# A two-layer hybrid block on one core: weight splits moved into the pair work, column sums folded on VectorE, y scaled on ScalarE, ada units moved

## The chip, the core and the metric

The kernel runs on 1 core of one Trainium2 chip. The time is that of one execution on the device, in microseconds. Below, the median of three runs is given, and beside it one execution that was taken with the hardware profiler. Times inside that execution count from the start of its span.

## What is computed

Two layers, on 512 tokens of 1024 channels, in fp32. Each layer is a mixer and a feed-forward part, each between two RMS norms and gated by values made from a condition vector c.

```python
def reference(...):
    c_act = jax.nn.silu(c)
    for l in range(DEPTH):
        mod = (c_act @ ada_w[l] + ada_b[l]).reshape(bsz, N_MOD, D_MODEL)[:, :, None, :]
        shift_m, scale_m, gate_m = mod[:, 0], mod[:, 1], mod[:, 2]
        shift_f, scale_f, gate_f = mod[:, 3], mod[:, 4], mod[:, 5]
        h = rms_norm(x, mix_pre_g[l]) * (1.0 + scale_m) + shift_m
        y = hybrid_mixer(h, ...)            # w_in, attention and RG-LRU, w_out
        x = x + gate_m * rms_norm(y, mix_post_g[l])
        h = rms_norm(x, ffn_pre_g[l]) * (1.0 + scale_f) + shift_f
        y = conv_ffn(h, ffn_w_up[l], ffn_conv_w[l], ffn_conv_b[l], ffn_w_down[l])
        x = x + gate_f * rms_norm(y, ffn_post_g[l])
    return x

def conv_ffn(h, w_up, conv_w, conv_b, w_down):
    u = causal_dwconv(h @ w_up, conv_w, conv_b)      # width 3 over time, 2 * 3072 channels
    g, val = jnp.split(u, 2, axis=-1)
    return (jax.nn.gelu(g, approximate=True) * val) @ w_down
```

## The kernel before

Channels lie on partitions in eight tiles, time (512) along the free dimension. A fp32 product is made of three fp32r products: of weight and activation each a high part (rounded) and a low part (the rest), high by high, high by low, low by high. The weights come as a stream of chunks of 128x1024, 512 KB each: per layer 14 for `w_in`, 8 for `w_out`, then three groups of 16 up chunks (gate and value alternate) and 8 down chunks. A chunk is loaded by SyncE into a ring of six slots (`refill`, L460, each load waits until the chunk six places before it has been used), ScalarE makes the high part (`split_step`, L595, into `wH`), and VectorE the low part (`lo_chunk`, L1149, in place as `wL`). The last two out chunks and the last two down chunks of each layer have side buffers of their own.

Every engine's order is written out by hand, and the engines meet by counting semaphores. TensorE's products are `half_products` (L1894, one half of 256 tokens) and `tile_products` (through `mm`, L1869, all 512). The out stage, the first six chunks of the up group and the last six down chunks are done in halves, so that the norms of the first half go on while TensorE does the second half. Two chunks of such a stage share one PSUM bank and are called a pair.

The places that the change touches:

- **Pair work.** The six chunks `U0` to `U0 + 5` are the gate and value chunks of three pairs. For each half h and pair p, ScalarE evicts both (`pair_base`, L828), VectorE adds the taps of the convolution (`pair_taps`, L1612 and L1614), ScalarE makes the gelu (`pair_gelu`, L836), VectorE the product (`pair_product`, L1629), ScalarE its high part (`pair_high`, L842) and VectorE its low part (`pair_low`, L1638). The prediction counts up chunks from one: chunk seven is `U0 + 6`, the first that is done in one piece. The splits of chunks seven to eleven stand between these steps, on ScalarE and VectorE alike. They are asked for by `ring_next(U0 + c, SLOTS_W - 1)`, the chunk five places on.
- **The later up chunks** run through a loop (`f_base`, L1049; taps, L1733 and L1736; gelu, L1045; high part, L1055; low part, L1745). A down chunk waits for the high and low part of each of its eight tiles.
- **Ada units.** `mod` is made in layer 0 for both layers, by VectorE: a unit is one row block of `ada_w`, 512 KB, fetched by GpSimd (L563), multiplied with c and summed (`dot_unit`, L1155). The table `UNITS` says after which chunk each unit is done.
- **Post norm.** The squares of y are summed over the tiles in `sum_of[h]`, whose 512 columns hold two sets of 256 tokens side by side (for the down stage tiles 0 and 1 are in `sum_full`). `post_early` on TensorE sums them over the partitions with matmuls against a column of ones (`half_sums`, L1994), 128 tokens at a time; `post_final` does the same with the last pair's squares. Then come ScalarE's root (`post_root`, L621), VectorE's reciprocal (L1199), and `post_spread`, which spreads the factor over the partitions (L1869). A matmul of plain fp32 is two instructions in the trace.
- **x_update** (L1205 to L1215) multiplies y by that factor and adds it to x, four tiles at a time. In the out stage y has been scaled by `fac` in its eviction, so one multiply does it (L1209); in the down stage `fac` is applied here, tile by tile (L1212). In the last layer the result is stored by SyncE (L511).

```python
for p in range(3):
    if p == 0:
        split_step(ring_next(U0 + 1, SLOTS_W - 1))
    pair_base(1, p)
    for c in range(2 * p, 2 * p + 2):
        if c > 1:
            split_step(ring_next(U0 + c, SLOTS_W - 1))
    pair_gelu(1, p)
    pair_high(1, p)
```

Of the kernel before, what the change touches and what calls it, by code (L numbers as in the profile page):

```python
# [25 lines left out]
P = 128  # L26
# [71 lines left out]
def build(nc, A):  # L98
# [3 lines left out]
    with ctx:  # L102
# [29 lines left out]
        side_raw = [at(f"side{i}", [P, KT * P], top[0] - (2 - i) * KT * SEQ * 4 + 4 * SEQ * 4) for i in range(2)]  # L132
        raw_at = top[0]
# [158 lines left out]
        fac_ready, last_ready = sem("fac_ready"), sem("last_ready")  # L292
# [51 lines left out]
        def norm_half(l, k, h):  # L344
            return 2 * (2 * l + k) + h + 1

# [66 lines left out]
        for _g in range(GROUPS):  # L413
            for _p in range(GRP // 2 if _g == 0 else 0, KT):
                _n = 2 if _g == 0 and _p < GRP else 1
                UNITS[up_no(_g, 2 * _p + 1)] = list(range(_u, _u + _n))
                _u += _n
# [25 lines left out]
        def _(sp):  # L443
# [63 lines left out]
            for h in range(2):  # L507
                for q in range(2):

                    sp.wait_ge(x_half, 2 * (norm_half(DEPTH - 1, 1, h) - 1) + q + 1)  # L510
                    sp.dma_start(out4[:, 4 * q:4 * q + 4, part_of(h)],  # L511
                                 x4[:, 4 * q:4 * q + 4, part_of(h)]).then_inc(stored, 16)
            sp.wait_ge(stored, 16 * 4)
# [70 lines left out]
        def _(act):  # L584
# [119 lines left out]
            for l in range(DEPTH):  # L704
# [98 lines left out]
                def out_evict(h, i):  # L803

                    if h == 0 and i == 0:
                        act.wait_ge(fac_ready, l + 1)
# [214 lines left out]
                pair_base(0, 2)  # L1021
                pair_gelu(0, 2)
# [3 lines left out]
                for p in range(3):  # L1026
                    if p == 0:
                        split_step(ring_next(U0 + 1, SLOTS_W - 1))
                    pair_base(1, p)
                    for c in range(2 * p, 2 * p + 2):  # L1030
                        if c > 1:
                            split_step(ring_next(U0 + c, SLOTS_W - 1))
# [31 lines left out]
                N0 = B + NCH  # L1064
                act.wait_ge(dn_read, dn_no(l, GROUPS - 1, 0))
# [5 lines left out]
                split_step(D0 + 7)  # L1071

                def down_squares(h, i):
# [10 lines left out]
                    else:  # L1084
                        nc.scalar.activation(two(last_sq[h]), src, ACT.Square).then_inc(last_ready, 1)

# [45 lines left out]
        def _(dve):  # L1132
# [44 lines left out]
            def factors(l, which):  # L1177
# [8 lines left out]
                else:  # L1186
                    link(TT(fac[:, l, which, :], m, g, ALU.mult))

            def add_square(l, k, s, h):
# [3 lines left out]
                dve.wait_ge(sq_used, add_no(l, k, s))  # L1193

# [6 lines left out]
            def x_update(l, k, h, q):  # L1201
# [6 lines left out]
                if k == 0:  # L1208
# [6 lines left out]
                TT(xs, xs, ys, ALU.add).then_inc(x_half, 1)  # L1215
# [120 lines left out]
            for l in range(DEPTH):  # L1336
# [313 lines left out]
                dve.sem_inc(post_summed, 1)  # L1650
# [17 lines left out]
                dve.sem_inc(post_summed, 1)  # L1668
# [844 lines left out]
```

## Time and profile before

| | |
|---|---|
| median of 3 runs | 1194.88 us (1192.77 to 1198.26) |
| the profiled execution | 1199.15 us |
| its span, first to last instruction | 1197.3 us |
| mean granted TensorE clock | 0.981 of full |
| TensorE matmul busy | 1165.3 us, 97% |
| TensorE weight load busy | 1016.3 us, 85% |
| VectorE busy | 821.9 us, 69% |
| ScalarE busy | 544.4 us, 45% |
| GpSimd busy | 52.1 us, 4% |
| read from HBM | 152.64 MB, 129 GB/s over the span |

The time of an execution is a little more than its span. A busy share is an average over stages: what ends a wait at one place is read from the timeline there. "PE" is TensorE, "DVE" VectorE, "ACT" ScalarE, "POOL" GpSimd and "SPq" SyncE's DMA issues. An entry in brackets at the end of a timeline row gives the idle time of the engine just before it, and what ended that.

### The profile page before, as it was taken

Reading aid. Unit: us, or ns where it says so; the run is one execution under the profiler, and the core shown is the slowest. Engines: PE = TensorE matmul, PEld = TensorE weight load, DVE = VectorE, ACT = ScalarE, POOL = GpSimd, SP = SyncE. Lnnn points to the kernel's source line nnn. Section 1 sums busy time; section 2 is a strip of 40 time slices with the busy share of each in tenths; the row PEclk is TensorE's granted clock in tenths of the full one; section 3 lists DMA queues with packets and bytes.
Section 4 is the critical chain, followed back from the end, with each engine's and each line's share of the span. In section 5 each row is a group of like instructions: output and inputs, shape, how many; then the busy total and the mean of one; then the engine's idle time right before and its main releaser. Section 6 shows DMA issues by size and latency. Waiting matters only on the chain.

```text
span 1197.3 us, 16181 instructions
## 1 busy us (share of the span) xinstructions
PE 1165.3 (97%) x6616; PEld 1016.3 (85%) x6616; DVE 821.9 (69%) x1267; ACT 544.4 (45%) x896; POOL 52.1 (4%) x110
## 2 busy tenths in 40 slices
PE   6999999989999999999999999998999999999996
PEld 6986899978788888888999779997888888888896
DVE  7899867688777777677487885577653666356634
ACT  5388726454224431444248874545432444234430
POOL 4000110000110011000000000000000000000000
PEclk8999889999999999999999999999999999999998
DMA  9833533235775458544113220304333333333312
GB/s 361 344 107 110 188 120 128 86 118 191 248 255 158 140 190 285 177 140 141 42 48 106 71 87 20 106 5 140 104 92 102 91 103 92 102 92 102 92 50 71
DMA packets 44938, 155.79 MB, mean 130 GB/s; under 512 B 5056, under 2 KB 7360, under 8 KB 44864
## 3 DMA queue, kind: packets, MB, share of 16 engines
q1 hardware_dynamic: 34352, 116.48, 29.5%
q0 software_dynamic: 10368, 37.75, 9.4%
q8 instruction: 52, 0.85, 0.3%
q10 hardware_dynamic: 144, 0.52, 0.1%
q14 instruction: 22, 0.18, 0.1%
HBM read 152.64 MB, written 2.10 MB: 129 GB/s over the span
## 4 chain that ended last, share of the span: by engine, by line
PE 80%; DVE 13%; ACT 4%; issue 2%; DMA 1%; SPq 0%; DVEq 0%
PE ps L1869 57%; PE ps L1894 21%; PE ps L1994 2%; DVE sb_wL L1149 2%; DVE sb_R L1614 1%; DVE sb_stage L1155 1%; ACT sb_R L828 1%; ACT sb_wH L595 1%; DVE sb_R L1736 1%; DVE sb_R L1733 1%; DVE sb_y L1233 1%; ACT sb_sq L700 1%; DVE sb_xc L1381 0%; DVE sb_adaw L1155 0%; DMA sb_raw<-in_w 0%
## 5 line engine op out<-in xcount | busy, mean ns | idle before, releaser
L1869 PE MATMUL ps<-sb_hH,sb_wH 128*128 128x512 f32 x800 | 315.3, 394 | 7.6 <-DVE sb_wL L1149 7.6
L1869 PE MATMUL ps<-sb_hH,sb_wL 128*128 128x512 f32 x800 | 312.1, 390 | 0.0
L1869 PE MATMUL ps<-sb_hL,sb_wH 128*128 128x512 f32 x800 | 311.9, 390 | 0.0
L595 ACT ACTIVATE sb_wH<-sb_raw 128x1024 fp32r<-128x1024 f32 x174 | 181.5, 1053 | 127.8 <-DMA sb_raw<-in_w 127.7
L1149 DVE TENSOR_TENSOR sb_wL<-sb_raw,sb_wH 128x1024 fp32r<-128x1024 f32 x174 | 211.7, 1219 | 30.3 <-ACT sb_wH L595 30.1
L1869 PEld LDWEIGHTS ps<-sb_hH,sb_wH 128*128 128x128 f32 x800 | 150.5, 188 | 42.0 <-DVE sb_wL L1149 9.1
L1869 PEld LDWEIGHTS ps<-sb_hL,sb_wH 128*128 128x128 f32 x800 | 150.6, 188 | 31.6 <-issue 1.0
L1869 PEld LDWEIGHTS ps<-sb_hH,sb_wL 128*128 128x128 f32 x800 | 150.5, 188 | 31.7
L1733 DVE SCALAR_TENSOR_TENSOR sb_R<-ps,sb_par,sb_R 128x511 f32<-128x511 f32 x84 | 62.9, 748 | 100.9 <-ACT sb_R L1049 100.7
L1049 ACT ACTIVATE sb_R<-ps,sb_par 128x512 f32<-128x512 f32 x84 | 65.2, 777 | 116.1 <-PE ps L1869 116.1
L1869 PE MATMUL ps<-sb_mH,sb_wH 128*128 128x512 f32 x288 | 112.1, 389 | 0.9 <-ACT sb_mH L1055 0.9
L1869 PE MATMUL ps<-sb_mL,sb_wH 128*128 128x512 f32 x288 | 112.2, 389 | 0.0
L1869 PE MATMUL ps<-sb_mH,sb_wL 128*128 128x512 f32 x288 | 112.1, 389 | 0.0
L1894 PE MATMUL ps<-sb_hH,sb_wH 128*128 128x256 f32 x384 | 104.3, 290 | 0.1
L1894 PE MATMUL ps<-sb_hH,sb_wL 128*128 128x256 f32 x384 | 102.9, 287 | 0.0
L1894 PE MATMUL ps<-sb_mH,sb_wH 128*128 128x256 f32 x320 | 94.6, 296 | 0.2 <-ACT sb_adaw L769 0.2
L1894 PE MATMUL ps<-sb_mL,sb_wH 128*128 128x256 f32 x320 | 92.4, 289 | 0.0
L1894 PE MATMUL ps<-sb_mH,sb_wL 128*128 128x256 f32 x320 | 92.4, 289 | 0.0
L1894 PE MATMUL ps<-sb_hL,sb_wH 128*128 128x256 f32 x384 | 80.9, 285 | 1.2 <-DVE sb_hL L1240 1.2
L1894 PEld LDWEIGHTS ps<-sb_hH,sb_wH 128*128 128x128 f32 x384 | 75.3, 196 | 0.2 <-issue 0.2
L1894 PEld LDWEIGHTS ps<-sb_hH,sb_wL 128*128 128x128 f32 x384 | 75.3, 196 | 0.0
L1055 ACT ACTIVATE sb_mH<-sb_I 128x512 fp32r<-128x512 f32 x42 | 26.5, 632 | 100.7 <-DVE sb_I L1743 100.7
(253 smaller groups left out, 1750.1 us busy)
## 6 DMA issues: line engine op xcount, KB each, us to landing
sb_raw<-in_w SPq DMA_DIRECT2D x174, 512.0 KB, 3.6
sb_adaw<-in_ada POOLq DMA_DIRECT2D x42, 512.0 KB, 4.7
sb_stage<-in_ada SPq DMA_DIRECT2D x24, 512.0 KB, 14.3
sb_vw<-in_ada POOLq DMA_DIRECT2D x20, 512.0 KB, 4.9
sb_side<-in_w SPq DMA_DIRECT2D x8, 512.0 KB, 4.9
sb_raw<-in_w SPq DMA_DIRECT2D x8, 384.0 KB, 14.3
sb_stage<-in_ada POOLq DMA_DIRECT2D x6, 512.0 KB, 4.1
sb_x<-in_x SPq DMA_DIRECT2D x4, 512.0 KB, 5.3
```

The lines of the kernel that those rows point to most:

```text
L595: nc.scalar.activation(high_of(n), raw_of(n), ACT.Copy).then_inc(w_hi, 1)
L700: last = nc.scalar.activation(swaps[rope_no(l, h, i) % 2][32 * q4:32 * q4 + 32, cols], pair_bank(h, i)[32 * o:32 * o + 32, cols], ACT.Copy)
L828: last = nc.scalar.activation(R[:, c % 4, part_of(h)], pair_bank(h, p)[:, (c % 2) * HALF:(c % 2 + 1) * HALF], ACT.Identity, bias=pcol(l, " ...
L1049: nc.scalar.activation(R[:, c % 4, :], bank(up_bank(u)), ACT.Identity, bias=par_l[:, COLS["fcb"] + col:COLS["fcb"] + col + 1], scale=pcol( ...
L1055: nc.scalar.activation(mH[:, p, :], I[:, 2 + p % 2, :], ACT.Copy).then_inc(act_hi, 1)
L1149: TT(low_of(n), raw_of(n), high_of(n).bitcast(fp32), ALU.subtract).then_inc(w_lo, 1)
L1155: STT(out=tile, in0=tile, scalar=1.0, in1=csb[:, :], op0=ALU.mult, op1=ALU.mult, accum_out=mod[:, seg, kt:kt + 1]).then_inc(ada_used, 1)
L1233: STT(out=yt(j)[:, part_of(h)], in0=xt(j)[:, part_of(h)], scalar=gains[:, j:j + 1], in1=bank(X_BANK[h])[:, 0:HALF], op0=ALU.mult, op1=ALU. ...
L1733: link(STT(out=buf[:, 1:], in0=acc[:, 0:SEQ - 1], scalar=pcol(l, "fcw", 2 * PAIRS + col), in1=buf[:, 1:], op0=ALU.mult, op1=ALU.add))
L1869: return nc.tensor.matmul(out, a, b, start=start, stop=stop, **kw)
L1894: return nc.tensor.matmul(out, a, b, start=start, stop=stop, skip_group_check=True)
L1994: return nc.tensor.matmul(out, a, b, start=start, stop=stop, skip_group_check=True)
```

## The change

Five things, all in the order or the operands of instructions.

1. On ScalarE and VectorE the split of chunk seven goes from behind the third pair of the first half to before its gelu (ScalarE) and before its product (VectorE). Chunk eight goes to the first pair of the second half, chunk nine stays with the second, ten and eleven stay with the third.
2. For the first halves (and the last layer's last half) VectorE adds `sum_full` (down stage) and the right 256 columns of `sum_of` onto the left 256 before TensorE sums over the partitions. `half_sums` then runs over one set of columns, and the matmuls on `sum_full` fall away.
3. In the last layer's down stage ScalarE writes y times `fac` into `scaled` (over hH and hL) beside its squares, and `x_update` has one multiply per four tiles instead of four.
4. The last half is stored in four pieces of two tiles instead of two of four, and its adds are split likewise.
5. Four ada units move from the first group's up chunks to the second's: pairs 4 to 8 of group 0 carried 2, 2, 2, 1, 1 and now carry 0, 1, 1, 1, 1; the first four pairs of group 1 now carry two each instead of one.

```diff
+        scaled = [at(f"scaled{i}", [P, 4, SEQ], top[0] - (2 - i) * KT * SEQ * 4) for i in range(2)]
...
+        def folded(l, k, h):
+
+            return h == 0 or (k == 1 and l == DEPTH - 1)
...
-            for _p in range(GRP // 2 if _g == 0 else 0, KT):
-                _n = 2 if _g == 0 and _p < GRP else 1
+            for _p in range(KT // 2 if _g == 0 else 0, KT):
+                _n = 2 if _g == 1 and _p < KT // 2 else 1
...
-            for h in range(2):
-                for q in range(2):
-
-                    sp.wait_ge(x_half, 2 * (norm_half(DEPTH - 1, 1, h) - 1) + q + 1)
-                    sp.dma_start(out4[:, 4 * q:4 * q + 4, part_of(h)],
-                                 x4[:, 4 * q:4 * q + 4, part_of(h)]).then_inc(stored, 16)
-            sp.wait_ge(stored, 16 * 4)
+            halves = 2 * (norm_half(DEPTH - 1, 1, 0) - 1)
+            for q in range(2):
+                sp.wait_ge(x_half, halves + q + 1)
+                sp.dma_start(out4[:, 4 * q:4 * q + 4, part_of(0)], x4[:, 4 * q:4 * q + 4, part_of(0)]).then_inc(stored, 16)
+            for q in range(4):
+                sp.wait_ge(x_half, halves + 2 + q + 1)
+                sp.dma_start(out4[:, 2 * q:2 * q + 2, part_of(1)], x4[:, 2 * q:2 * q + 2, part_of(1)]).then_inc(stored, 16)
+            sp.wait_ge(stored, 16 * 6)
...
-                        act.wait_ge(fac_ready, l + 1)
+                        act.wait_ge(fac_ready, 2 * l + 1)
...
                 pair_base(0, 2)
+                split_step(ring_next(U0 + 1, SLOTS_W - 1))
                 pair_gelu(0, 2)
...
                 for p in range(3):
-                    if p == 0:
-                        split_step(ring_next(U0 + 1, SLOTS_W - 1))
                     pair_base(1, p)
-                    for c in range(2 * p, 2 * p + 2):
-                        if c > 1:
-                            split_step(ring_next(U0 + c, SLOTS_W - 1))
+                    for c in ((2,), (3,), (4, 5))[p]:
+                        split_step(ring_next(U0 + c, SLOTS_W - 1))
                     pair_gelu(1, p)
...
+                def scale(j, part):
+
+                    if l == DEPTH - 1:
+                        nc.scalar.activation(scaled[j // 4][:, j % 4, part], yt(j)[:, part], ACT.Copy,
+                                             scale=fac[:, l, 3, j:j + 1]).then_inc(y_scaled, 1)
...
+                if l == DEPTH - 1:
+                    act.wait_ge(fac_ready, 2 * l + 2)
+                scale(0, slice(0, SEQ))
+                scale(1, slice(0, SEQ))
...
                         nc.scalar.activation(two(last_sq[h]), src, ACT.Square).then_inc(last_ready, 1)
+                    scale(2 + 2 * i, part_of(h))
+                    scale(3 + 2 * i, part_of(h))
...
+            def all_added(l, k, h):
+
+                if folded(l, k, h):
+                    first = sum_of[h][:, 0:HALF]
+                    if k == 1:
+                        link(TT(first, first, sum_full[:, part_of(h)], ALU.add))
+                    link(TT(first, first, sum_of[h][:, HALF:2 * HALF], ALU.add))
+                dve.sem_inc(post_summed, 1)
...
-                if k == 0:
+                final = k == 1 and l == DEPTH - 1
+                if final:
+                    ys = scaled[q][:, :, part_of(h)]
+                    dve.wait_ge(y_scaled, 2 + 6 * h + (2 if q == 0 else 6))
+                if k == 0 or final:
                     V.mark(TT(ys, ys, rb.unsqueeze(1).broadcast_to([P, 4, HALF]), ALU.mult))
...
-                TT(xs, xs, ys, ALU.add).then_inc(x_half, 1)
+                if final and h:
+                    for j in range(2):
+                        two = slice(2 * j, 2 * j + 2)
+                        TT(xs[:, two, :], xs[:, two, :], ys[:, two, :], ALU.add).then_inc(x_half, 1)
+                else:
+                    TT(xs, xs, ys, ALU.add).then_inc(x_half, 1)
...
                 add_square(l, 0, 1, 0)
-                dve.sem_inc(post_summed, 1)
+                all_added(l, 0, 0)
...
-                half_sums(h, 0, sum_of[h], k == 1, False)
-                if k == 1:
+                half_sums(h, 0, sum_of[h], k == 1, False, 1 if folded(l, k, h) else 2)
+                if k == 1 and not folded(l, k, h):
```

VectorE's pair work gets the same new places with `lo_chunk` for `split_step`; `all_added` stands wherever `post_summed` was raised.

ScalarE in layer 0, from the eviction of the first half's third pair on, before (`sb_wH` is a split, `w_in2` the slot of chunk seven, `w_in3` that of eight; two evictions, gelu and high part make a pair):

```order
L828 ACTIVATE sb_R<-ps,sb_par 128x256 [waits p_mul,half_done]
L828 ACTIVATE sb_R<-ps,sb_par 128x256
L836 ACTIVATE sb_I<-sb_R 128x256 [waits p_taps]
L842 ACTIVATE sb_mH<-sb_I 128x256 [waits p_mul]
L1025 DMA sb_gw<-in_gw 128x1024
L595 ACTIVATE sb_wH<-sb_raw 128x1024 [waits w_in2]
L828 ACTIVATE sb_R<-ps,sb_par 128x256 [waits chunk_done]
L828 ACTIVATE sb_R<-ps,sb_par 128x256
L836 ACTIVATE sb_I<-sb_R 128x256 [waits p_taps]
L842 ACTIVATE sb_mH<-sb_I 128x256 [waits p_mul]
L828 ACTIVATE sb_R<-ps,sb_par 128x256 [waits chunk_done]
```

and in the change:

```order
L834 ACTIVATE sb_R<-ps,sb_par 128x256 [waits p_mul,half_done]
L834 ACTIVATE sb_R<-ps,sb_par 128x256
L601 ACTIVATE sb_wH<-sb_raw 128x1024 [waits w_in2]
L842 ACTIVATE sb_I<-sb_R 128x256 [waits p_taps]
L848 ACTIVATE sb_mH<-sb_I 128x256 [waits p_mul]
L1032 DMA sb_gw<-in_gw 128x1024
L834 ACTIVATE sb_R<-ps,sb_par 128x256 [waits chunk_done]
L834 ACTIVATE sb_R<-ps,sb_par 128x256
L601 ACTIVATE sb_wH<-sb_raw 128x1024 [waits w_in3]
L842 ACTIVATE sb_I<-sb_R 128x256 [waits p_taps]
L848 ACTIVATE sb_mH<-sb_I 128x256 [waits p_mul]
```

The split of chunk seven has passed one gelu and one high part, and that of chunk eight stands one pair earlier.

VectorE at the end of the last layer, from the last add of squares on, before (`sb_scr` is `sum_of[1]` and, in its right half, `sum_full`):

```order
L1192 TENSOR_TENSOR sb_scr<-sb_scr,sb_sq 128x512 [waits sq_ready]
L1775 TENSOR_TENSOR sb_y<-ps,sb_y 128x2x256 [waits sq_used,chunk_done]
L1199 RECIPROCAL sb_tiny<-sb_tiny 128x2 [waits post_sd]
L1212 SCALAR_TENSOR_TENSOR sb_y<-sb_y,sb_fac,ps 128x256 [waits post_rb]
L1212 SCALAR_TENSOR_TENSOR sb_y<-sb_y,sb_fac,ps 128x256 x3
L1215 TENSOR_TENSOR sb_x<-sb_x,sb_y 128x4x256 [waits dve_self]
```

and in the change:

```order
L1210 TENSOR_TENSOR sb_scr<-sb_scr,sb_sq 128x512 [waits sq_ready]
L1218 TENSOR_TENSOR sb_scr<-sb_scr 128x256 [waits sq_used]
L1219 TENSOR_TENSOR sb_scr<-sb_scr 128x256 [waits dve_self]
L1809 TENSOR_TENSOR sb_y<-ps,sb_y 128x2x256 [waits dve_self,chunk_done]
L1226 RECIPROCAL sb_tiny<-sb_tiny 128x2 [waits post_sd]
L1240 TENSOR_TENSOR sb_scaled_62<-sb_scaled_62,ps 128x4x256 [waits y_scaled,post_rb]
L1249 TENSOR_TENSOR sb_x<-sb_x,sb_scaled_62 128x2x256 [waits dve_self]
L1249 TENSOR_TENSOR sb_x<-sb_x,sb_scaled_62 128x2x256
```

Two folding adds stand ahead of the last pair's own add, one multiply stands for four, and two adds for one. The second group of four tiles follows in the same way.

## Rows read from the trace of the kernel before

**Rows 1.** The page: busy time by engine, and the chain that ended last.

```profile
PE 1165.3 (97%) x6616; PEld 1016.3 (85%) x6616; DVE 821.9 (69%) x1267; ACT 544.4 (45%) x896; POOL 52.1 (4%) x110
...
PE 80%; DVE 13%; ACT 4%; issue 2%; DMA 1%; SPq 0%; DVEq 0%
```

**Rows 2.** Waits of TensorE: us in total, times, longest us.

```profile
PE ps L1869 <- DVE sb_wL L1149: 7.6, 4, 2.2
...
PE ps L2129 <- DVE sb_mL L1429: 1.5, 1, 1.5
PE ps L1894 <- DVE sb_hL L1240: 1.2, 2, 1.1
```

**Rows 3.** Timeline, pair work of layer 0: start us, us, engine, line, operation.

```profile
233.75 1.01 ACT L828 ACTIVATE sb_R<-ps,sb_par 128x256 f32<-128x256 f32 x2
236.61 0.42 ACT L836 ACTIVATE sb_I<-sb_R 128x256 f32<-128x256 f32 x1 [1.85 <-DVE sb_R L1614]
...
237.94 1.06 ACT L595 ACTIVATE sb_wH<-sb_raw 128x1024 fp32r<-128x1024 f32 x1
...
240.31 0.50 PE L1869 MATMUL ps<-sb_hH,sb_wH 128*128 128x512 f32 x1 [1.63 <-DVE sb_wL L1149]
...
244.65 2.00 ACT L595 ACTIVATE sb_wH<-sb_raw 128x1024 fp32r<-128x1024 f32 x2
...
247.00 2.35 DVE L1149 TENSOR_TENSOR sb_wL<-sb_raw,sb_wH 128x1024 fp32r<-128x1024 f32 x2
...
248.27 0.50 PE L1869 MATMUL ps<-sb_hH,sb_wH 128*128 128x512 f32 x1 [2.20 <-DVE sb_wL L1149]
```

**Rows 4.** Line L460, loads issued at 230.8 and, fourth of the burst, 233.0.

```profile
DMA to landing us min/median/max: 3.7/3.7/3.7
...
DMA to landing us min/median/max: 6.2/6.2/6.2
```

**Rows 5.** Windows: us, then busy by engine, TensorE's granted clock, DMA share, GB/s.

```profile
238.70:254.05 15.35, 11.53 (x49) 9.23 (x50) 12.48 (x32) 8.91 (x16) 0.00 (x0) 1.00 0.37 126
254.05:264.93 10.88, 10.88 (x49) 9.01 (x48) 8.79 (x12) 5.86 (x9) 0.00 (x0) 1.00 0.30 97
297.56:304.42 6.86, 5.98 (x25) 4.35 (x25) 5.50 (x8) 3.23 (x5) 0.53 (x1) 1.00 0.44 153
814.50:831.30 16.80, 13.13 (x49) 10.36 (x50) 14.10 (x34) 8.74 (x16) 0.00 (x0) 0.90 0.23 77
...
823.90:827.30 3.40, 3.39 (x9) 2.73 (x10) 2.43 (x6) 1.94 (x4) 0.00 (x0) 0.59 0.17 69
138.60:158.90 20.30, 20.25 (x94) 19.13 (x95) 8.63 (x17) 6.06 (x13) 3.14 (x6) 0.50 0.41 144
```

**Rows 6.** First group of layer 0: the chain in order of time, then TensorE's timeline.

```profile
275.56 1.14 DVE sb_vw L1155 x2
...
285.87 1.14 DVE sb_adaw L1155 x2
...
303.17 0.50 PE L1869 MATMUL ps<-sb_mH,sb_wH 128*128 128x512 f32 x1 [0.88 <-ACT sb_mH L1055]
```

**Rows 7.** First half's sums, layer 0 down stage: the chain, then VectorE's timeline.

```profile
588.27 1.23 PE ps L1994 x12
...
588.31 0.69 DVE L1775 TENSOR_TENSOR sb_y<-ps,sb_y 128x512 f32<-128x512 f32 x1 [3.67 <-PE ps L1894]
```

**Rows 8.** Timeline of the tail, layer 0's out stage at 185.45, and the last store.

```profile
185.45 1.22 DVE L1209 TENSOR_TENSOR sb_y<-sb_y,ps 128x1024 f32<-128x1024 f32 x1 [1.19 <-PE ps L1869]
...
1186.50 0.26 ACT L621 ACTIVATE sb_tiny<-ps,sb_tiny 128x2 f32<-128x2 f32 x1 [1.14 <-PE ps L1994]
...
1188.27 1.66 DVE L1212 SCALAR_TENSOR_TENSOR sb_y<-sb_y,sb_fac,ps 128x256 f32<-128x256 f32 x4 [1.31 <-PE ps L1869]
1189.96 1.23 DVE L1215 TENSOR_TENSOR sb_x<-sb_x,sb_y 128x1024 f32<-128x1024 f32 x1
...
DMA to landing us min/median/max: 2.9/2.9/2.9
```

More of the change, by code:

```diff
@@ L291, in build @@
         post_rs, post_rb = sem("post_rs"), sem("post_rb")
-        fac_ready, last_ready = sem("fac_ready"), sem("last_ready")
+        fac_ready, last_ready, y_scaled = sem("fac_ready"), sem("last_ready"), sem("y_scaled")
         x_half, xsq_ready, x_summed = sem("x_half"), sem("xsq_ready"), sem("x_summed")
@@ L1187, in factors @@
                     link(TT(fac[:, l, which, :], m, g, ALU.mult))
+                    dve.sem_inc(fac_ready, 1)
             def add_square(l, k, s, h):
@@ L1667, in _ @@
                 add_square(l, 0, 3, 1)
-                dve.sem_inc(post_summed, 1)
+                all_added(l, 0, 1)
                 tmp_half(l, 0, 0, 2)
@@ L1712, in _ @@
                 pair_taps(0, 2)
+                lo_chunk(ring_next(U0 + 1, SLOTS_W - 1))
                 pair_product(0, 2)
@@ L1715, in _ @@
                 for p in range(3):
-                    if p == 0:
-                        lo_chunk(ring_next(U0 + 1, SLOTS_W - 1))
                     pair_taps(1, p)
-                    for c in range(2 * p, 2 * p + 2):
-                        if c > 1:
-                            lo_chunk(ring_next(U0 + c, SLOTS_W - 1))
+                    for c in ((2,), (3,), (4, 5))[p]:
+                        lo_chunk(ring_next(U0 + c, SLOTS_W - 1))
                     pair_product(1, p)
@@ L1790, in _ @@
                 add_square(l, 1, 1, 0)
-                dve.sem_inc(post_summed, 1)
+                all_added(l, 1, 0)
                 down_half(0, 2)
@@ L1799, in _ @@
                     add_square(l, 1, 2, 1)
-                    dve.sem_inc(post_summed, 1)
+                    all_added(l, 1, 1)
                     down_half(1, 2)
@@ L1815, in _ @@
                 add_square(l, 1, 2, 1)
-                dve.sem_inc(post_summed, 1)
+                all_added(l, 1, 1)
                 x_recip(l, 1, 0)
@@ L1994, in part_mm, with half_sums @@
                 return nc.tensor.matmul(out, a, b, start=start, stop=stop, skip_group_check=True)
-            def half_sums(h, at_, src, opens, closes):
+            def half_sums(h, at_, src, opens, closes, parts=2):
                 for t in range(2):
-                    for g in range(2):
+                    for g in range(parts):
                         first = g * HALF + t * P
                         last = part_mm(bank(STAT_BANK[h])[:, at_ + t:at_ + t + 1], src[:, first:first + P], ones[:, 0:1],
-                                       opens and t == 0 and g == 0, closes and g == 1)
+                                       opens and t == 0 and g == 0, closes and g == parts - 1)
                 return last
```

## Prediction

> **What bounds the kernel now.** I read the page's busy shares and chain first, then the waits of TensorE, then its timeline around each wait, then the windows. TensorE is busy for 1165.3 of 1197.3 us, and 80% of the chain that ended last is its own work [rows 1]. So time is won where TensorE stands still, where its clock is low, and where it runs matmuls that another engine could replace; work saved elsewhere counts only in the tail, after the last product. The largest wait is for one line, the low split of a weight chunk: 7.6 us in 4 waits, two per layer [rows 2].
>
> The timeline of layer 0 shows why [rows 3]. TensorE reaches up chunk seven at 238.68 and waits 1.63 us. ScalarE rounded its weights at 237.94 only, though the chunk's load, issued at 230.8, had landed after 3.7 us, at 234.5 [rows 4]: the split stood behind gelu and high part of the third pair. Then TensorE waits 2.20 us for chunk eight: ScalarE splits eight and nine together at 244.65, after the second pair's eviction, and VectorE ends the low split of eight at 248.2 (the row at 247.00 holds both). The data had been there for long, so both are waits for a place in ScalarE's order. Layer 1 repeats them.
>
> **Part 1, the splits.** The honest price is the time that two chunks take. From the end of chunk six to that of chunk eight (SyncE's loads mark these ends) layer 0 needs 15.35 us; the next two chunks need 10.88, or 5.44 each [rows 5]. Lost: 4.47. In layer 1 it is 16.80, lost 5.92, of which some 1.6 is the clock: after the second wait TensorE is granted 0.59 for 3.4 us [rows 5], which is mostly 1.2 instead of 2.4 GHz. Together 10.4 us; besides waits and clock, each restart costs a few tenths.
>
> Do the waits vanish or only move? I replay layer 0 with the durations of its rows. ScalarE ends the eviction of the third pair at 234.76 [rows 3], and the chunk is there (234.5). Split of seven 234.7 to 235.7; VectorE ends this pair's taps at 236.6 as before, then the low split to 237.7. Needed at 238.68: 1.0 us to spare. Product, high and low part of the pair follow 1.1 us later than they did. Eviction of the second half's first pair to 239.5, split of eight to 240.4, taps to 241.9, low split to 243.0; needed at 238.68 + 5.44 = 244.1. Next pair: low split of nine ends 248.2, needed at 249.6. Then ten at 253.4 for 255.0, eleven at 254.6 for 260.4. The least margin is 1.0 us. What is queued behind the moved split is the gelu of the same pair, which in both kernels waits for the taps until 236.61 anyway [rows 3]. Term: **10.4 us**; bounds 5 (one wait of each pair reappears) and 10.4.
>
> **Part 2, units moved.** In layer 0 each ada unit takes 1.14 us of VectorE, and a pair of chunks with two of them 10.3 us, from 275.56 to 285.87 [rows 6]. Before, three pairs of the first group carry two units, and VectorE stays behind until TensorE waits at 303.17 for the last high part, 0.88 us [rows 6]; that down chunk takes 6.86 instead of 5.44 [rows 5], so 1.42 is lost. Four units leave this group: 4 x 1.14 = 4.6 us of VectorE, and its first step starts 1.1 us earlier by the replay. The high part would be ready 5.7 us earlier, and TensorE needs it 4.47 us earlier. So it just fits, with a margin near 1.2 - 0.88 = 0.3 us. Term: **1.4 us**; bounds 0 and 1.4. The four units land in group 1, where four pairs now carry two. Such a pair takes VectorE 10.3 us against TensorE's 10.88 [rows 5, 6]: no new wait. GpSimd's fetches of the same units wait for their slots and move with them; two per pair of chunks is less than the two per chunk of the down chunks.
>
> **Part 3, column sums.** A sum matmul is issued as two passes: twelve instructions take 1.23 us, 0.10 apiece [rows 7]. Folding takes away 4 instructions in the out stage and 8 in the down stage, in each of 2 layers: 24 x 0.10 = **2.4 us** on TensorE. The last layer's second half loses 8 too, but there TensorE waits for the square of the last pair anyway: nothing. VectorE gains one add of 128x256 per out stage and two per down stage, some 0.4 us each as half of the 0.69 for 128x512 [rows 7]. Their cover is VectorE's pause of 3.67 us before the next half pair [rows 7]; without it they would delay the root and all that follows by 0.4 to 0.9 us a time. Bounds of the term: 1.5 and 2.5.
>
> **Part 4, the tail.** After the last spread everything is on the path: per group of four tiles 1.66 us of scaling and 1.23 of adding, twice [rows 8]. With y scaled beforehand the scaling is one multiply, as in the out stage, 1.22 [rows 8]: 0.44 saved each time. Each add becomes two, which costs an extra start: four pieces take 1.66 where one takes 1.22, so about 0.1 each. Net 0.7. ScalarE's two new scalings of the last pair stand ahead of its root; the eviction of two 128x256 pieces at 233.75 took 1.01 [rows 3], and ScalarE pauses 1.14 us there [rows 8]: hidden, barely. If they take longer, the excess is on the path. The last store holds 256 instead of 512 KB. 512 KB landed after 2.9 us [rows 8]; four loads issued within 2.2 us landed after 3.7 to 6.2 us [rows 4], so about 1.55 apart, which is what 512 KB costs in flow. Half is 0.75; the store before it, 0.6 earlier, takes back 0.1. Saved 0.65. Term: **1.3 us**, bounds 0.3 and 2.
>
> The loads of [rows 4] overlap everything but the flow of data, and two more stores should do so too. The Trainium skill, DMA: Bandwidth & Descriptors, Anatomy of one DMA, speaks against more and smaller transfers: it gives each about 2.0 us of fixed cost beside its bytes. Paid one after another, by its figures the last store would land 1.7 us later than now, and the sum would be 13.2.
>
> **Sum.** 10.4 + 1.4 + 2.4 + 1.3 = 15.5 us. Against the profiled execution (span 1197.3, time 1199.15) this gives 1183.6. The median of the runs shown is 4.3 lower, 1194.88. Whether the clock fell in layer 1 in those runs too is not known, so I take half of the 1.6: 14.7, and **1180.2 us**. Its own range is 1177 to 1183.5.
>
> **Rivals.**
> A, the waits move on. The replay has 1.0 us to spare, and loads further back in a burst landed up to 2.5 us later than the first [rows 4]; a late one now holds the whole pair work of ScalarE. Half of the 10.4 returns: 1185.4. For it: the thin margins. Against: the first of the burst is the one in question, and all later chunks have more.
> B, the last two stores run one after another with their whole 2.9 us each [rows 8]: the last lands 2 x 2.9 - 0.6 = 5.2 us after its issue, 2.3 later than now, where I counted 0.65 earlier. The sum is 12.6, the time 1183.1. Against it: the overlap in [rows 4].
> C, the clock. In this trace TensorE runs at 0.50 from 138.60 to 158.90 [rows 5]; at full clock that work would take half, so 10.2 us. It followed a wait of 1.5 us [rows 2], while a wait of 1.63 at 240.31 [rows 3] cost no clock. The change moves nothing there, but shifts all that follows, and waits remain, as at 643 us for the second half's hL [rows 2]. One such stretch more: 1190.4. The Trainium skill, TensorE: Matmul & The Clock Gate, Part 1, says that where the clock changes differs between runs of one kernel. One execution with a profile can neither bear that out nor refute it.
> D, the other side. The same mechanism in layer 1 behind 643 us, where scores, transposes and projections alternate with pauses until 720. Each stretch costs 10.2; two leave the kernel at 1200.6, within half a per cent of before, and slower by over 0.5% begins at 20.7 us lost. Three give 1210.8. Against: this part ran at 1.00 before, and its own order does not change.
> That the change doesn't do what it says is hardly open: the instruction order shows the splits ahead of gelu, and the sums gone.
>
> **Chances.** Forecast 0.72, A 0.14, B 0.04, C 0.07, D 0.03. A measurement of this kernel can tell about 0.5% from no change, 6.0 us, so faster means below 1188.9: forecast, A and B, 0.90. C is the same, 0.07, D slower, 0.03. The range of 1176.5 to 1187.5 takes in A and B, the smaller bounds of parts 2 to 4, and the upper side of the clock; C and D stay out.
>
> **What would show it.** Right: TensorE's waits for the low split at chunks seven and eight gone in both layers, two chunks in 10.9 us there, clock 1.00 in the first group of layer 1; no wait at the first down chunk of layer 0; first-half sums of 2 + 4 and 4 instructions instead of 10 and 12; two scaling multiplies of 1.22 at the end, and a last landing near 2.2 us after its issue. Wrong: a wait of over 1 us for chunks seven to eleven (part 1), one near the last high part (part 2), a root of the last half later than 1.1 us after its sums (part 4), or a new stretch below full clock.

## The result, and the profile after

| | before | changed |
|---|---|---|
| median of 6 runs | 1197.25 us (1192.77 to 1202.89) | 1185.53 us (1174.32 to 1187.11) |
| ratio, 95% interval | | 0.988 (0.983 to 0.993) |
| the profiled execution | 1199.15 us | 1174.32 us |
| its span, granted clock | 1197.3 us, 0.981 | 1172.5 us, 0.992 |

The change is faster by 1.2%, 0.7 to 1.7%. The forecast of 1180.2 us lies 5.3 below the median, inside its range of 1176.5 to 1187.5. But the two profiled executions are 24.8 us apart and the medians 11.7, where the sum said 15.5. Both deviations come mainly of stretches in which TensorE's clock is at half, and which differ from execution to execution; five of the twelve experiments are about them.

The page of the changed kernel:

```profile
PE 1149.5 (98%) x6584; PEld 1003.1 (86%) x6584; DVE 823.1 (70%) x1265; ACT 550.0 (47%) x910; POOL 51.9 (4%) x110
...
PE 90%; DVE 7%; ACT 1%; issue 1%; DMA 1%; SPq 0%; DVEq 0%
```

TensorE has 32 instructions fewer than in [rows 1]: the 24 first-half sums of part 3 and the 8 of the last half. Its own work is 90% of the chain now, against 80.

Its waits (us in total, times, longest):

```profile
PE ps L2163 <- DVE sb_mL L1465: 1.5, 1, 1.5
PE ps L2028 <- ACT sb_sqo L1100: 1.1, 1, 1.1
PE ps L1928 <- DVE sb_hL L1276: 1.1, 1, 1.1
```

The 7.6 us for `wL` in [rows 2] are gone. The 1.1 us for `sqo` stands where the last half's sums did; it is the tail's wait for the last squares, foreseen under part 3.

The timeline of layer 0's pair work, three engines (start us, us, engine, line, operation), beside [rows 3]:

```profile
224.61 1.00 ACT L834 ACTIVATE sb_R<-ps,sb_par 128x256 f32<-128x256 f32 x2
225.51 1.06 ACT L601 ACTIVATE sb_wH<-sb_raw 128x1024 fp32r<-128x1024 f32 x1
...
227.35 1.22 DVE L1166 TENSOR_TENSOR sb_wL<-sb_raw,sb_wH 128x1024 fp32r<-128x1024 f32 x1
...
227.46 0.42 ACT L842 ACTIVATE sb_I<-sb_R 128x256 f32<-128x256 f32 x1 [0.90 <-DVE sb_R L1650]
...
229.38 0.40 PE L1903 MATMUL ps<-sb_hH,sb_wH 128*128 128x512 f32 x1
...
230.27 1.06 ACT L601 ACTIVATE sb_wH<-sb_raw 128x1024 fp32r<-128x1024 f32 x1
...
232.64 1.22 DVE L1166 TENSOR_TENSOR sb_wL<-sb_raw,sb_wH 128x1024 fp32r<-128x1024 f32 x1
```

The split of chunk seven follows the eviction at once. Its low part ends at 228.57, and TensorE begins the chunk at 229.38 with no wait: 0.8 us to spare, where the replay had 1.0. The gelu still waits 0.90 us for the taps, so the split in front of it delays nothing.

Windows (us, then busy by engine, TensorE's granted clock, DMA share, GB/s): chunks seven and eight of layer 0, the next two, the first down chunk, seven and eight of layer 1, and the stretch at 139 us.

```profile
229.58:240.49 10.91, 10.91 (x49) 9.01 (x48) 8.55 (x23) 5.97 (x12) 0.00 (x0) 1.00 0.53 182
240.49:251.37 10.88, 10.88 (x49) 9.01 (x48) 9.45 (x18) 5.88 (x9) 0.00 (x0) 1.00 0.28 97
284.01:289.50 5.49, 5.49 (x25) 4.42 (x24) 4.16 (x6) 3.09 (x5) 0.00 (x0) 1.00 0.50 185
798.19:809.10 10.91, 10.91 (x49) 9.01 (x49) 8.55 (x23) 5.96 (x12) 0.00 (x0) 1.00 0.43 149
138.60:158.90 20.30, 19.97 (x170) 19.37 (x170) 16.32 (x30) 11.17 (x20) 3.66 (x7) 1.00 0.44 157
```

Against [rows 5]: 15.35 and 16.80 us are now 10.91 each, 6.86 is 5.49, and the stretch at 139 us ran at 1.00 in this execution where the one before ran at 0.50.

The chain in layer 0's down stage has the first half's sums, twelve in [rows 7], as

```profile
573.35 0.34 PE ps L2028 x4
```

And the tail, VectorE and ScalarE, with the landing of the last store, beside [rows 8]:

```profile
1163.43 0.26 ACT L627 ACTIVATE sb_tiny<-ps,sb_tiny 128x2 f32<-128x2 f32 x1 [0.34 <-PE ps L2028]
...
1164.79 1.22 DVE L1240 TENSOR_TENSOR sb_scaled<-sb_scaled,ps 128x1024 f32<-128x1024 f32 x1 [0.89 <-PE ps L1903]
1166.04 1.29 DVE L1249 TENSOR_TENSOR sb_x<-sb_x,sb_scaled 128x512 f32<-128x512 f32 x2
...
DMA to landing us min/median/max: 2.3/2.3/2.3
```

The root still waits for TensorE, by 0.34 us: ScalarE's two scalings are hidden, barely. The multiply takes 1.22 instead of 1.66.

**Where the 24.8 us went.** Aligned by SyncE's loads, the two spans differ by 9.7 in the part of layer 0 that holds the stretch at 139 us and the out stage (9.3 of it clock, 0.4 the out stage's sums), 4.4 and 5.9 in the pair works, 1.4 at the first down chunk, 0.9 + 0.4 + 0.9 in the other three first-half sums, and 1.75 in the tail; the start took 0.6 more. (The 0.4 of layer 0's out stage is taken from layer 1's, where no clock fall hides it.) The terms of the prediction are thus 16.1 of the 24.8, and the clock at 139 us is 9.3, which no part of the change addresses.

### The profile page after: what moved, and what is told of

Same layout as the page of the kernel before. It is cut to its first block, busy times and chain, and to the rows that moved or that the text cites. A ratio compares the mean times of both kernels' runs of the same rounds, so it can differ in the third digit from the quotient of the medians.

```text
span 1172.5 us, 16135 instructions
## 1 busy us (share of the span) xinstructions
PE 1149.5 (98%) x6584; PEld 1003.1 (86%) x6584; DVE 823.1 (70%) x1265; ACT 550.0 (47%) x910; POOL 51.9 (4%) x110
## 4 chain that ended last, share of the span: by engine, by line
PE 90%; DVE 7%; ACT 1%; issue 1%; DMA 1%; SPq 0%; DVEq 0%
PE ps L1903 64%; PE ps L1928 24%; PE ps L2028 2%; DVE sb_stage L1172 1%; DVE sb_wL L1166 1%; DMA sb_raw<-in_w 1%; ACT sb_sq L706 1%; DVE sb_xc L1417 1%; DVE sb_tiny L1399 0%; PE ps L2163 0%; ACT sb_scr L706 0%; DVE sb_scr L1303 0%; DVE sb_mL L1465 0%; DVE sb_R L1430 0%; DMA sb_sq<-in_pos 0%
## 6 DMA issues: line engine op xcount, KB each, us to landing
sb_raw<-in_w SPq DMA_DIRECT2D x8, 384.0 KB, 14.4
```

## The experiments

All runs have their own executions of the kernel before beside them on the same chip: with those of the result 64 in all, 1190.7 to 1202.9, median 1197.7 (the ratios are each against its own). The change had 12 executions in two runs, median 1185.4; where a run is compared with "the change" below, it is with these or with the profiled one.

**Each part alone: the splits back.** The change with the old places of the splits on both engines:

```diff
-                split_step(ring_next(U0 + 1, SLOTS_W - 1))
                 pair_gelu(0, 2)
...
                 for p in range(3):
+                    if p == 0:
+                        split_step(ring_next(U0 + 1, SLOTS_W - 1))
                     pair_base(1, p)
-                    for c in ((2,), (3,), (4, 5))[p]:
-                        split_step(ring_next(U0 + c, SLOTS_W - 1))
+                    for c in range(2 * p, 2 * p + 2):
+                        if c > 1:
+                            split_step(ring_next(U0 + c, SLOTS_W - 1))
```

> The changed kernel with the splits of chunks seven to eleven where they were. Theory (the terms add, each wait is one for its place in the order): TensorE waits again for chunk seven, some 1.5 us, and chunk eight, some 2.2 us, in both layers; from the end of chunk six to that of eight 15 us instead of 10.9 in layer 0 and 15 to 17 in layer 1; 9 to 10.4 us slower than the change at the same clock. Rival (the clock): the gain of the changed kernel came mainly from a stretch at half clock that it happened not to have; then this kernel is slower by under 4 us at the same clock. Of the first down chunk of layer 0: with the units moved but TensorE late again it must not wait.

Measured: 1194.58 us (10 runs), ratio 0.998 (0.995 to 1.001): without the splits hardly anything of the gain is left that a median can tell. The waits are back, in both layers; the windows are chunks seven and eight of each, then the first down chunk of layer 0:

```profile
235.11:250.42 15.31, 11.54 (x49) 9.23 (x50) 12.47 (x32) 8.89 (x16) 0.00 (x0) 1.00 0.38 124
809.58:824.77 15.19, 11.50 (x49) 9.23 (x50) 12.46 (x32) 8.76 (x16) 0.00 (x0) 1.00 0.26 89
293.94:299.38 5.44, 5.44 (x25) 4.50 (x24) 3.52 (x5) 3.04 (x4) 0.00 (x0) 1.00 0.33 108
```

The pair works took 4.40 and 4.28 us more than in the change, 8.7 together, at a clock of 1.00 in both. That is a little under the 9 to 10.4 expected at equal clock, and far above the rival's 4. The rest of the 10.4 is the fall of the clock in layer 1 of [rows 5], which did not occur in this execution. The first down chunk takes 5.44 without a wait, where [rows 5] had 6.86: beside the old splits the moved units are worth 1.42.

**The units back.**

```diff
-            for _p in range(KT // 2 if _g == 0 else 0, KT):
-                _n = 2 if _g == 1 and _p < KT // 2 else 1
+            for _p in range(GRP // 2 if _g == 0 else 0, KT):
+                _n = 2 if _g == 0 and _p < GRP else 1
```

> The changed kernel with the old table of units (2, 2, 2, 1, 1 for the last five pairs of group 0). Theory: TensorE is 4.4 us further ahead than before, VectorE gains 1.1 us only, so the wait for the last high part at the first down chunk of layer 0 is not 0.9 but some 4.3 us, and that is the whole loss: 4 to 5 us slower than the change at the same clock. Rival (the unit term is its own 1.4 us, whatever the splits do): 1.4 us slower.

Measured: 1190.3 us (10 runs), ratio 0.994 (0.991 to 0.998). TensorE's waits show one that neither kernel has:

```profile
PE ps L1903 <- ACT sb_mH L1059: 4.1, 1, 4.1
```

and the windows of the first down chunk and of the next one show its price:

```profile
295.63:306.14 10.51, 6.41 (x25) 4.92 (x24) 8.89 (x12) 5.85 (x8) 0.53 (x1) 0.89 0.35 101
306.14:313.77 7.63, 7.63 (x25) 6.02 (x25) 5.89 (x10) 1.22 (x2) 1.58 (x3) 0.71 0.61 183
```

Two chunks that take 11.0 us took 18.1: 4.1 of wait, and 3 because the clock was at half from 303.7 to 310.5, from the end of the wait on. The expectation had the wait right and left this fall out. So the units are worth 7.2 us in this execution, where the same move is worth 1.4 beside the old splits; the medians differ by 4.9 (1190.3 against 1185.4).

**The splits without the units.** The kernel before with the new places of the splits only; the edit is that of the change's first part.

> The kernel before with the new places of the splits of chunks seven to nine, and nothing else of the change. Theory (the splits are worth their full price only together with the moved units): TensorE's waits for chunks seven and eight go in both layers, and the stretch of the two chunks is 10.9 us in each. In layer 1 that gives 4.3 us at full clock. In layer 0 TensorE is then earlier by 4.4 us at the first down chunk, but VectorE with its old share of units is not, and TensorE waits some 4 to 5 us there for the last high part, where it waited 0.88; layer 0 keeps under 1 us of its gain. So about 5 us at the same clock, 4 to 6, against about 12 for splits and units together; if the clock falls after that wait, less by about 3. Rival (the prediction's reading, each part with its own price): 8.7 to 10.4 us, with a wait under 1.5 us at the first down chunk.

Measured: 1193.09 us (10 runs), ratio 0.997 (0.995 to 0.999). Both pair works take 10.91, and the first down chunk 10.54, with a wait of 4.14 us; the chunk behind it takes 7.63 because of the clock:

```profile
238.42:249.33 10.91, 10.91 (x49) 9.01 (x49) 8.56 (x23) 5.96 (x12) 0.00 (x0) 1.00 0.52 173
815.58:826.49 10.91, 10.91 (x49) 9.01 (x49) 8.57 (x23) 5.97 (x12) 0.00 (x0) 1.00 0.37 116
292.85:303.39 10.54, 6.40 (x25) 4.91 (x24) 8.92 (x12) 5.87 (x8) 0.53 (x1) 0.89 0.37 113
303.39:311.02 7.63, 7.63 (x25) 6.02 (x25) 5.90 (x10) 1.23 (x2) 1.58 (x3) 0.71 0.61 173
```

The splits alone win 4.4 us of median. That fits the stages: 10.3 won at the pair works, and 3.7 and 2.1 lost again at these two down chunks. The rival, each part with a price of its own, falls.

**The sums back.** `folded` returns False everywhere.

```diff
-            return h == 0 or (k == 1 and l == DEPTH - 1)
+            return False
```

> The changed kernel without the folding adds, TensorE sums both sets of columns and sum_full again. Theory: 24 instructions of 0.10 us on TensorE's path, 2.4 to 2.7 us slower at the same clock, as steps of 0.4 and 0.9 us at the out and the down stage of each layer; in the tail nothing. Rival (VectorE's adds are on the path too, or the sums were hidden): under 1 us.

Measured: 1186.08 us (5 runs), ratio 0.991 (0.987 to 0.994). The median alone can't tell it from the change. The stages can: the one with layer 0's first-half down sums takes 118.79 instead of 117.88, 0.91 for eight instructions. The last layer's takes 0.9 more too, and from the last reciprocal to the end nothing changes but the clock of the last spread. The two out stages stand where the clock fell in this execution; beside the kernel before, layer 1's shows 0.45. The rival, under 1 us in all, falls.

**The tail back**, scaling and stores:

```diff
-                    if l == DEPTH - 1:
+                    if False:
                         nc.scalar.activation(scaled[j // 4][:, j % 4, part], yt(j)[:, part], ACT.Copy,
...
-                if k == 0 or final:
+                if k == 0:
...
-            for q in range(4):
+            for q in range(2):
```

> The changed kernel with y scaled by VectorE in the last x_update, whole adds and two stores for the last half. Theory: 0.44 us twice for scaling less 0.1 twice for the split adds, and 0.65 for the store: from the end of the last spread to the end of the span 1.3 us longer, nothing else moves. Rival (the two more stores cost their own 2 us one after another): the tail here is shorter by 1 us or more.

Measured: 1179.28 us (4 runs), ratio 0.986 (0.982 to 0.990), so a lower median than the change had, with a tail that is longer: from the last reciprocal to the end 10.56 us against 8.79. That is no gain from undoing the tail; it is the first sign that medians of few runs do not compare like with like here.

Its two halves were then undone one by one.

> The change with only the scaling of y by fac taken back: VectorE again multiplies tile by tile, four instructions of 128x256, in the last layer too; the last half's stores stay four. Theory: from the last reciprocal to the end 8.77 + 2 x 0.44 = 9.65 us, some 0.9 more than in the change, with the first of those groups at 1.66 instead of 1.22. Rival (the scaling on ScalarE costs on the way to the root what it saves behind it): no difference from the last product to the end, since the root would come 0.9 us earlier without ScalarE's two scalings.

> The change with only the last half's stores and adds taken back to two of four tiles. Theory: the last add 0.14 us earlier (1.23 in place of 0.69 + 0.68), the last landing 0.65 to 0.9 later after its issue (2.9 in place of 2.2 us), so from the last reciprocal to the end 8.77 + 0.5 to 0.8 = 9.3 to 9.6. Rival (a transfer's fixed time is nearly all of it, so that size does not matter): the last landing at the same 2.2 us or so after its issue, and the end within 0.2 us of the change's.

The two medians (1182.91 and 1181.14 us, two executions each) tell nothing of this size. Measured, from the last reciprocal to the end: 9.57 with the scaling back, 9.69 with the stores back. One thing must be taken off: VectorE's wait for the last spread differs with the clock at that place, 0.80 and 1.32 us against 0.89 in the change, and 1.32 with the whole tail back. Scaling: 0.78 + 0.09 = 0.87. Stores: 0.90 - 0.43 = 0.47. The whole tail: 1.77 - 0.43 = 1.34, their sum. The scaling's rows, and the landing of the last 512 KB:

```profile
1173.56 1.65 DVE L1240 SCALAR_TENSOR_TENSOR sb_y<-sb_y,sb_fac,ps 128x256 f32<-128x256 f32 x4 [0.80 <-PE ps L1900]
```

```profile
DMA to landing us min/median/max: 2.9/2.9/2.9
```

A landing of 2.9 for 512 KB and 2.3 for 256 gives 0.6; each add that is made in two pieces takes 0.07 more (1.29 against 1.22), twice, which leaves 0.46, the 0.47 above. The rival that size doesn't matter falls, and so does the one that the scaling costs on the way to the root what it saves: from VectorE's last add to the root it is 2.5 us with the scaling on ScalarE and without.

**The clock at 139 us.** The first six executions of the change had 1174.3 and 1177.6 us at a clock of 0.99, and 1184.9 to 1187.1 at 0.98. All seven experiments so far had, in their profiled execution, a slow stretch that began at 138 to 141 us, behind TensorE's wait of 1.5 us for the fourth transposes. The wait was filled with work that nothing uses:

```diff
                     attn_products(0, 3)
+                    for _ in range(7):
+                        mm(bank(5), nil[:, :], nil[:, 0:1].broadcast_to([P, SEQ]), True, True)
                     probs_transposed(3)
```

> The change with seven more fp32r matmuls of 128x512 on TensorE, on zeros into a bank that is free there, right ahead of the fourth set of transposes in layer 0's attention, where TensorE otherwise stands still for 1.5 us at about 137 us. They add work that nothing uses. Theory (the time of this kernel has two levels because TensorE's clock falls to half in a stretch that begins at 138 to 140 us, after that wait, in some executions and not in others): without the standstill the stretch does not begin, the clock is 0.99 in all or nearly all executions, and the median is 1174 to 1178, against 1185 for the change; the filling itself costs under 0.3 us. Rival (the stretch comes of the work of that stage as a whole, or of what the chip does otherwise, not of that one wait): the stretch begins there as before in more than half of the executions, and the median stays within 2 us of 1185.5.

Measured: 1178.59 us, 1174.2 to 1179.3 and once 1186.2. That one was the profiled execution, and it shows where its stretch began (windows of TensorE alone):

```profile
138.00:142.40 4.40, 4.07 (x35) 1.00 0.00 0
142.40:159.50 17.10, 17.10 (x82) 0.50 0.51 184
```

The wait at 137 is filled, yet the clock fell 3 us later than in the change, behind the short wait of 0.33 for the copied transposes and among sums of one column. The median is lower by 7, but the stretch still occurs, so neither expectation held whole, and the change itself had to be run again beside it, with a kernel that fills more, three matmuls each behind `outputs_mm(3)`, `attn_cols(3)` and the second `lru_cols`:

> The change itself, unaltered, as the yardstick for the two runs beside it on the same chip. The first six executions of the change had 1174.3 and 1177.6 us with a mean clock of 0.99, and 1184.9 to 1187.1 with 0.98. If the share of executions with the slow stretch belongs to the kernel: again more than half at 1184 to 1187, median near 1185. If it belongs to the chip or the hour (the change with its tail undone had no execution above 1181.7, with 1.8 us more work): mostly 1174 to 1180, median near 1178, and then the 1178.6 of the kernel with fillers is no gain of theirs.

> The change with the seven filler matmuls ahead of the fourth set of transposes, and three more behind each of three groups of one-column sums in the 8 us that follow; nine more cost 9 x 0.24 = 2.2 us, less what they fill. Theory (the slow stretch begins because TensorE has too little to do in this stage, and the wait at 137 is only a part of that; the stretch after the seven fillers began at 142.4, behind the next short wait): with the whole stage filled the stretch never begins, all executions lie within 2 us of each other, at 1176 to 1179, clock 0.99 or more. Rival (the stretch does not depend on what TensorE does in this stage): executions at 1186 to 1189 are seen as often as with seven fillers or none.

> The kernel with seven fillers once more, to be compared with the change on the same chip: the first time one of six executions had the slow stretch in full (1186.2), the others lay at 1174.2 to 1179.3. Theory (the fillers make the stretch shorter or rarer): median 1176 to 1180, and at least 4 us below that of the change beside it. Rival (no effect): both medians within 2 us.

| on one chip | median | executions | mean granted clock |
|---|---|---|---|
| the change again | 1184.83 | 1178.1, 1182.1, 1183.7, 1185.9, 1187.2, 1187.5 | 0.979 to 0.988 |
| seven fillers again | 1178.22 | 1174.8, 1176.5, 1177.3, 1179.2, 1182.5, 1184.0 | 0.982 to 0.992 |
| sixteen fillers | 1177.75 | 1176.3, 1176.9, 1177.0, 1178.5, 1178.7, 1179.7 | 0.989 to 0.992 |

The sixteen fillers' executions lie 3.4 us apart, where 2 was expected. The profiled one with seven (1174.76) had no stretch, and between the loads around the stage it took 47.35 us, the change without a stretch 47.39: these seven cost nothing.

The change again, profiled at 1187.22 us:

```profile
134.00:138.00 4.00, 2.48 (x21) 1.00 0.00 0
138.00:139.50 1.50, 1.36 (x14) 1.00 0.00 0
139.50:160.00 20.50, 20.32 (x94) 0.50 0.39 139
```

With sixteen fillers, at 1176.29:

```profile
134.00:138.00 4.00, 4.00 (x30) 1.00 0.00 0
139.50:160.00 20.50, 20.50 (x168) 1.00 0.42 155
```

Last, the seven fillers where they fill nothing, behind the stage's last narrow sums:

```diff
                     lru_cols(3, True)
+                    for _ in range(7):
+                        mm(bank(5), nil[:, :], nil[:, 0:1].broadcast_to([P, SEQ]), True, True)
                     attn_products(1, 0)
```

> The change with the same seven filler matmuls, but behind the stage's last one-column sums at about 147.5 us, where TensorE has wide products on both sides and no wait to fill: they lengthen the stage by 7 x 0.24 = 1.7 us. Theory (what counts is that TensorE is filled at the wait and among the narrow sums, before 142 us): the slow stretch begins at 138 to 142 us in most executions as in the change, and the median is that of the change plus about 1.7, so 1185 to 1188, with some executions at 1186 to 1189. Rival (any seven more matmuls or any shift of the later work by a microsecond does it): the median at 1177 to 1181, as with the fillers ahead.

Measured: 1181.33 us, three executions at 1177.0 to 1179.5 and three at 1183.1 to 1185.1, where the theory had 1185 to 1188 and the rival 1177 to 1181. Its mean clocks, 0.983 to 0.991, are close to those of the seven fillers ahead. So the theory that the place is what counts is not borne out, though six executions cannot refute it either. What its profile shows is the old fall at the old place, ahead of the fillers:

```profile
134.00:137.90 3.90, 2.38 (x23) 1.00 0.00 0
137.90:151.50 13.60, 13.45 (x63) 0.50 0.52 194
```

Counted as executions more than 6 us above the lowest of their kernel: before 38 of 64, the change 9 of 12, fillers behind 3 of 6, seven fillers ahead 3 of 12, sixteen 0 of 6. That the kernel with sixteen fillers has the stretch less often than the change is shown: on the one chip where both ran side by side it is 5 of 6 against 0 of 6, and no execution of either has a mean clock in the other's range. Why is not shown: not that the filled wait of 1.5 us or the narrow sums behind it are the cause, and not even that the fillers must stand ahead of 142 us, since the run with seven behind came out with nearly the clocks of the one with seven ahead. Sixteen matmuls elsewhere were not tried.

The kernel with sixteen fillers has the lowest median, 1177.75 us, ratio 0.984 (0.982 to 0.987) to the kernel before, 7.1 us under the change beside it, though it does more work: its profiled span at full clock is 1174.5, 2.0 longer than the change's.

## Why the prediction was right

**Part 1, the splits: 10.4 forecast, 10.3 found** between the two profiles (4.4 and 5.9), 8.7 of it standstill and restart, the rest the clock fall that layer 1 of the profiled execution before happened to have. The replay held, its margin of 1.0 us came out as 0.8. Rival A, late loads that bring the waits back in these chunks, did not occur; that they did not move on to the first down chunk is owed to part 2.

**Part 2, the units: 1.4 forecast, 1.37 found** (6.86 to 5.49). The step that it rests on was read rightly: the high part had to be ready 4.47 us earlier, by its working it would be by 5.7, and no wait was seen. What the prediction failed to say is that its terms are not additive. Without the units the 4.47 gained in layer 0 come back as a wait of 4.1 us, plus 3 for the clock. So 1.4 is right as a term of this sum, and wrong as the price of the part: taken out of the change, it costs 7.2.

**Part 3, the sums: 2.4 forecast, 2.7 found.** Instructions that were counted at 0.10 apiece are worth 0.11: eight of them gave 0.90, four 0.45. Chain [rows 7] gives 0.1025 by division, but the four that stay take 0.34, so the eight that went took 0.89. That no more than this was won or lost in these stages says that VectorE's folding adds were covered.

**Part 4, the tail: 1.3 forecast, 1.34 found** at equal clock, 0.87 of scaling (0.88 forecast) and 0.47 of stores and split adds (0.65 less 0.2 forecast; 0.6 less 0.14 found). Another 0.4 between the two profiles is a last spread that ran partly at full clock. Rival B falls: the last two stores were issued 0.6 us apart and each landed after 2.2 or 2.3 us. The rule of the Trainium skill that stood behind it (DMA: Bandwidth & Descriptors, Anatomy of one DMA: about 2.0 us fixed for each transfer, measured there for those that GpSimd issues) is near for these single ones of SyncE: 2.3 for 256 KB and 2.9 for 512 leave an estimated 1.7 without bytes. But here the fixed parts of two transfers overlap.

**The sum: 15.5 forecast, 16.1 found** between the two profiles. Both hold 1.6 of clock in layer 1, and the 16.1 also the 0.4 at the last spread, so at equal clock it is 13.9 against 14.1. The many executions agree: wherever some of both kernels have the same mean granted clock (0.981, 0.982, 0.983, 0.984, 0.988 and 0.990), their averages are 12.8 to 14.4 us apart. And the mean of the 12 of the change is 13.6 below that of the 64 before.

**Rival C, the clock,** described what decides the rest, though not as it was priced. It was put as one more stretch that the change might bring, against a fixed one at 139 us, at 10.2 us. In truth the one at 139 us comes and goes in both kernels, and it costs 9.3. The weak step is the tie from the sum to the median. It took the median of three executions for the kernel's level, and let the median of the change lie below it by the sum, less half of the 1.6 of layer 1; with executions spread over 12 us and more, medians of three and six do not hold still to that. The rule of the Trainium skill cited there (TensorE: Matmul & The Clock Gate, Part 1: where the clock changes differs between runs) agrees with the profiles: the stretch began at 137.9 to 142.4 us or not at all, and twelve executions of one and the same kernel spread over 13.2 us. Of the 5.3 by which the median missed, 2.9 is the first yardstick: three runs of before with 1194.88, against 1197.7 for all 64. The other 2.5 is where the median of six fell: four of them had a mean clock of 0.979 to 0.982, and the mean of the same six is 1182.8. The change had the stretch in 9 of 12 by the count above, the kernel before in 38 of 64; 12 executions are too few to tell these shares apart, so that part of the miss is best called chance.

## What to carry to other kernels

Price parts of a change together when one brings TensorE earlier to a place where another engine has its own backlog: here the units were worth 1.4 us beside the old splits and 7.2 beside the moved ones, and the splits alone won 4.4 us where the stages of splits and units together gave 11.7 (1.6 of it clock). Compare like with like by stages between fixed marks (loads are good ones), at equal granted clock, before reading a median of a few runs; and where the executions of a kernel spread widely, compare those of equal mean clock and look for the stretch that differs. Useless work on TensorE can be worth more than it costs: here sixteen matmuls lengthened the work by 2.0 us and lowered the median by 7.1. It has to be tried, since what they prevent is not understood.

## What was not expected of the hardware

- The clock fall behind 138 us begins at 138 to 142 us and lasted 13.65, 17.07 or 20.48 us, or did not occur. Between the loads around it, it cost 5.8 to 6.1 us, 7.7 or 7.8, and 9.2 or 9.3, somewhat less than half of its length. It moves the time of this kernel more than three of the four parts of the change do.
- With a wait of 4.1 us at 300 us the clock fell to half for 6.8 us in both kernels that had it, 0.7 us before the wait ended. Waits of 1.6 and 2.2 us in layer 0's pair work cost no clock in either kernel, and the 2.2 us in layer 1 did in one execution (3.41 us) and not in another.
- Short falls of 3.41 us to half clock also stand where no wait is ahead of them, as at 204 and 610 us in the repeated run of the change, where they cost 1.5 us each. They were seen only in executions that had the long stretch at 139 us too, though not in all of those. In all eleven such falls TensorE had run 16 to 24 sums of one column within the 4 us before; in the other executions the same sums ran and the clock stayed. What brings them stays open; it wasn't tried.
